# A chunked delta-rule recurrence: turning the inverse's T on VectorE in 32 by 32 blocks, and both directions' products in turn

## The chip, the cores and the metric

The kernel is one program on one core of a Trainium2 chip. The metric is the device time of one execution in microseconds (us). The engines are TensorE (PE; its weight loads are PEld), VectorE (DVE), ScalarE (ACT), GpSimd (POOL) and SyncE (SP), which issues the DMAs here.

## The reference

One layer of a diffusion backbone over 512 latent tokens behind 256 context tokens, in float32: a projection into two token mixers (pooling and a bidirectional RWKV-7 recurrence), a gated merge, and a mixture of experts. Only the recurrence matters here. For each of 16 heads of 64 channels and for both directions it is, token by token:

```python
def step(s, inp):
    r_t, w_t, k_t, v_t, kk_t, b_t = inp
    sa = jnp.einsum('bhvk,bhk->bhv', s, -kk_t)
    s = s * w_t[:, :, None, :] + sa[..., None] * b_t[:, :, None, :] + v_t[..., None] * k_t[:, :, None, :]
    return s, jnp.einsum('bhvk,bhk->bhv', s, r_t)
```

It runs over the context from a zero state and from there over the latent tokens; the second direction runs in reverse.

## The kernel before

The recurrence is worked in chunks of 64 tokens: four of context (0 to 3) and eight latent ones (4 to 11), each with both directions d = 0 and 1. Inside a chunk the steps become matrix products, with the inverse of a 64 by 64 unit triangular matrix per head, T. T begins as the identity with the first off-diagonals (unit T1) and is built up in five levels b = 2, 4, 8, 16, 32: G is a product of the chunk's rows Z with T, X is a product of G with T turned, and a masked copy puts the part of X that belongs to the level into T.

The work of each chunk is a list of units (`recurrence_units`), each with a PSUM bank pair in rotation: unit n takes slot n % 4 and may begin when the reader of unit n - 4 is done (`begin`, `wait_read`). The units are Z (rows of the next chunk, four parts), BKt and Vt (operands turned by a product with the identity), G2 to G32, Tr1 to Tr16 (T turned by TensorE), X2 to X32, and, for the chunk before, P (products with the state), XTr (turned), U (the solved values), Y (output) and S (state update). TensorE goes through them in the written order; chunk i's inverse is interleaved with chunk i - 1's P to S and chunk i + 1's Z. ScalarE and VectorE each read their units in the order of the same list (`by_act`, `by_dve`), and each engine's semaphore (`pe_s`, `act_s`, `dve_s`) counts them.

ScalarE copies Z, Vt (two copies of 64 partitions per direction), BKt, P, XTr, U, every G and every Tr from PSUM to SBUF. VectorE makes T1 (`dve.transpose` of Z in 32 by 32 blocks and a masked copy), the masked copies of X2 to X16 into T, the turned T for the last level (Tf) with X32's masked copy, half of each U, Y's addition and the state update S (an addition and a product with `decay_end`). GpSimd fills T with the identity, clears UV and multiplies Z by its masks once ScalarE has copied it. SyncE loads the rows of the next chunks.

Matrices of 64 by 64 use a quarter of TensorE's array: its row half is given by the operands' partitions, its column half by the output's. `OWN` is the pair of halves of partitions. In G and X the four combinations of row and column half follow one another within one direction, and the row half also picks the PSUM bank of the pair.

## Time and profile before

| what | value |
|---|---|
| median of 3 runs | 1524.66 us (1523.47 to 1525.41) |
| the profiled execution's own time | 1523.53 us |
| its span | 1521.0 us |
| PE busy | 1328.0 us, 87% of the span, 16500 instructions |
| DVE busy | 620.2 us, 41% |
| ACT busy | 578.9 us, 38% |
| POOL busy | 235.3 us, 15% |

The span is the time from the first to the last instruction on the core; the execution's own time holds what lies around it. In the timeline of an engine each row is a run of like instructions: its start, its length from the first start to the last end, the line of the kernel, the operation with output and inputs, the number of instructions, and in brackets how long the engine had stood idle and what ended that. A TensorE matmul of 32-bit data appears as two records, so 32 instructions of G count as x64; the turns with the identity appear once. A row in which the next begins before the first has ended is no error: instructions are pipelined, and start to start is the pace.

### The profile page before, as it was taken

The page shows a single profiled execution, that of the slowest core. Times are in us where ns is not written, and L with a number is a line of the kernel's source. Part 1 is how long each engine was busy: PE and PEld are TensorE (multiplying, and loading weights), DVE is VectorE, ACT ScalarE, POOL GpSimd, SP SyncE. Part 2 cuts the span into 40 slices and gives each one's busy share as a digit, 9 for nine tenths or more (in the row PEclk, how much of TensorE's full clock was granted, in tenths as well). Part 3 has the DMA queues.
Part 4 walks back from the last instruction along what each step waited for, and adds up shares of the span by engine and source line. Part 5 has one row for each costly group of instructions (what it writes and reads, how often), then busy time and mean ns, then how long its engine had stood idle before and what let it go on. Part 6 is the DMA issues. An engine that isn't in the chain of part 4 may idle for free. (4 is left out here: it accounts for less than half of the span.)

```text
span 1521.0 us, 37771 instructions
## 1 busy us (share of the span) xinstructions
PE 1328.0 (87%) x16500; PEld 797.3 (52%) x16500; DVE 620.2 (41%) x974; ACT 578.9 (38%) x964; POOL 235.3 (15%) x191
## 2 busy tenths in 40 slices
PE   5889999999999999999998788999999468788780
PEld 3445555554888888888887233444445323222220
DVE  1247777674555445454444451523321510000014
ACT  4235445542665656556654530000003223322233
POOL 0011111220322333333330000000000011100002
PEclk9999999999999999999999899999999679989895
DMA  9204565645222222112200529453454659999984
GB/s 379 90 1 139 159 174 177 185 123 177 106 86 73 100 67 84 67 71 83 80 29 23 229 99 387 161 202 112 152 219 186 275 214 422 426 424 425 426 341 186
DMA packets 104697, 279.87 MB, mean 184 GB/s; under 512 B 20691, under 2 KB 69971, under 8 KB 90595
## 3 DMA queue, kind: packets, MB, share of 16 engines
q1 hardware_dynamic: 98596, 248.24, 44.0%
q0 software_dynamic: 5952, 29.36, 4.9%
q8 instruction: 127, 2.08, 0.5%
q14 instruction: 22, 0.18, 0.0%
HBM read 232.48 MB, written 53.49 MB: 188 GB/s over the span
## 5 line engine op out<-in xcount | busy, mean ns | idle before, releaser
L391 PE MATMUL pr_ps<-hT,pr_w 128*128 128x512 f32 x384 | 172.2, 602 | 4.0 <-DVEq L99 4.0
L972 DVE COPY_PREDICATED rc_T<-masks_sb,rc_ps 128x512 f32<-128x512 uint32 x96 | 65.2, 728 | 151.2 <-PE rc_ps L761 151.1
L391 PEld LDWEIGHTS pr_ps<-hT,pr_w 128*128 128x128 f32 x384 | 72.1, 191 | 94.9 <-issue 90.1
L1250 PE MATMUL mg_ps<-hT,mg_w 128*128 128x512 f32 x256 | 112.9, 600 | 2.7 <-PEq L1029 2.7
L1737 DVE TENSOR_TENSOR mg_w<-mg_w,ex_pgu 128x256 f32<-128x256 f32 x16 | 6.7, 421 | 194.5 <-ACT mg_w L1731 194.5
L1250 PEld LDWEIGHTS mg_ps<-hT,mg_w 128*128 128x128 f32 x256 | 49.1, 192 | 65.4 <-issue 65.4
L1269 ACT ACTIVATE mg_sig<-mg_ps 128x512 f32<-128x512 f32 x16 | 9.6, 597 | 188.1 <-PE mg_ps L1250 188.1
L761 PE MATMUL rc_ps<-rc_T,rc_Z 64*64 64x64 f32 x3840 | 73.4, 221 | 6.6 <-issue 5.3
L912 ACT ACTIVATE rc_G<-rc_ps 128x512 f32<-128x512 f32 x120 | 66.1, 599 | 23.5 <-PE rc_ps L761 23.0
L501 POOL TENSOR_TENSOR pr_kd<-pr_rate,pool_space 128x768 f32<-128x768 f32 x16 | 29.0, 1814 | 280.9 <-DVE pr_kraw L543 280.9
L734 PE MATMUL rc_ps<-masks_sb,rc_T 128*128 128x128 f32 x480 | 67.6, 281 | 4.8 <-DVE rc_Tf L970 4.8
L936 POOL TENSOR_TENSOR rc_Z<-rc_Z,masks_sb 64x512 f32<-64x512 f32 x48 | 64.9, 1352 | 42.5 <-ACT rc_Z L894 39.7
L761 PEld LDWEIGHTS rc_ps<-rc_T,rc_Z 64*64 64x64 f32 x3840 | 64.4, 135 | 12.7 <-issue 7.9
L894 ACT ACTIVATE rc_Z<-rc_ps 128x1024 f32<-128x1024 f32 (+1 forms) x48 | 41.5, 881 | 74.5 <-PE rc_ps L727 74.5
L914 ACT ACTIVATE rc_Tt<-rc_ps 128x512 f32<-128x512 f32 x120 | 66.8, 609 | 5.3 <-PE rc_ps L734 5.2
L1731 ACT ACTIVATE mg_w<-ex_pgu 128x256 f32<-128x256 f32 x16 | 6.1, 384 | 158.6 <-PE ex_pgu L1869 158.6
L1359 PE MATMUL po_ps<-pl_w_box,merged 128*128 128x512 f32 x128 | 59.5, 621 | 2.8 <-PEq L1205 2.8
L761 PE MATMUL rc_ps<-rc_G,rc_Tt 64*64 64x64 f32 x3072 | 57.4, 221 | 4.0 <-issue 2.3
L1727 ACT ACTIVATE hT<-ex_px,f_cols 128x128 f32<-128x128 f32 x128 | 46.5, 469 | 34.2 <-PE ex_px L1717 34.2
L1250 PE MATMUL mg_ps<-rwkv_y,mg_w 128*128 128x512 f32 x128 | 58.0, 607 | 0.0
L399 PE MATMUL pr_ps<-hT,pr_w 128*128 128x256 f32 x256 | 57.9, 379 | 0.0
L734 PEld LDWEIGHTS rc_ps<-masks_sb,rc_T 128*128 128x128 f32 x480 | 51.2, 141 | 11.0 <-DVE rc_Tf L970 6.4
(358 smaller groups left out, 2596.7 us busy)
## 6 DMA issues: line engine op xcount, KB each, us to landing
bonus_sb<-in_ada_w SPq DMA_DIRECT2D x16, 1024.0 KB, 7.0
mg_w<-in_w_merge SPq DMA_DIRECT2D x8, 1792.0 KB, 7.5
pr_w<-in_w_prep SPq DMA_DIRECT2D x8, 1664.0 KB, 9.8
kr_chunks<-pr_KR SPq DMA_DIRECT2D x16, 768.0 KB, 4.2
bk_chunks<-pr_BK SPq DMA_DIRECT2D x16, 768.0 KB, 6.5
rc_BK<-bk_chunks SPq DMA_DIRECT2D x24, 512.0 KB, 4.2
rc_KR<-kr_chunks SPq DMA_DIRECT2D x24, 512.0 KB, 4.2
rwkv_y<-in_w_experts SPq DMA_DIRECT2D x5, 2048.0 KB, 17.8
```

The source lines that it names most:

```text
L391: last = pe.matmul(lat_bank[:, :], wv[:, j * KT + kt, :], hT[:, kt, lat], start=(kt == 0), stop=(kt == KT - 1))
L399: last = pe.matmul(ctx_bank[:, 0:CTX], wv[:, j * KT + kt, :], hT[:, kt, 0:CTX], start=(kt == 0), stop=(kt == KT - 1))
L734: last = pe.transpose(out[:, q // Q, q % Q * P:q % Q * P + P], src(q), g["ident"])
L761: last = pe.matmul(out[to, k, q * C:q * C + C], lhs(at, q, s, b), rhs(at, q, s, b), start=True, stop=True)
L894: act.activation(Z[u][:, d // 2, :, at:at + Q, 0:w], src.rearrange("p b (j n) -> p b j n", n=P)[:, :, :, 0:w], ACT.Copy).then_inc(act_s, 1)
L912: act.activation(G[:, d, :, :, :], src[:, :, 0:Q * C].rearrange("p s (q t) -> p s q t", q=Q), ACT.Copy).then_inc(act_s, 1)
L914: act.activation(Tt[:, d, :, :, :], turned, ACT.Copy).then_inc(act_s, 1)
L936: pool.tensor_tensor(first, first, both[OWN[side], 0:C].unsqueeze(1).unsqueeze(1).to_broadcast([HD, 2, Q, C]), ALU.mult)
L972: dve.copy_predicated(T[u][:, d, :, :, :].rearrange("p q b t -> p b q t"), level(int(s[1:]), d), by_side).then_inc(dve_s, 1)
L1250: last = pe.matmul(ps[u][j][:, :], w[:, u, w0 + k, :], rhs, start=(k == 0), stop=(k == n - 1))
L1359: last = pe.matmul(ps[t % 2][:, half(h)], merged[:, k, t * P:t * P + P], w[:, k, half(h)], start=(k == 0), stop=(k == KT - 1))
L1727: last = act.activation(xT[:, v, k, :], p_x[:, k, :], ACT.Identity, scale=fcols[:, 0, k:k + 1], bias=fcols[:, 1, k:k + 1])
```

## The change

T is no longer turned by TensorE. After every level VectorE turns it in 32 by 32 blocks (units Tt2 to Tt32), directly behind the masked copy. For direction 0 that is one instruction; for direction 1 it is two, each of 64 partitions, that write the other half of the partitions. The ten Tr units of a chunk and their ScalarE copies are gone, as are Tf and its two turns; X32 is masked straight into the turned T (Tt). Because the two directions' operands or outputs now lie in opposite halves, the products G, X2 to X16 and U go through both directions in turn, and each waits for the second direction's inputs. A direction's outputs of both row halves now share a PSUM bank. X32 is still done direction by direction. The Vt units move from behind G2 to behind U, and U's second half is copied by ScalarE rather than VectorE.

```diff
-        out += front("G2") + front("Tr1") + front("Vt") + back("P")[0:1] + front("X2") + back("P")[1:2]
-        out += front("G4") + front("Tr2") + back("XTr") + front("X4") + back("U")
-        out += front("G8") + front("Tr4") + back("Y") + front("X8") + back("S") + rows_of(0, 1)
-        out += front("G16") + front("Tr8") + rows_of(2) + front("X16") + rows_of(3)
-        out += front("G32") + front("Tr16") + ahead("BKt") + front("X32")
+        out += front("G2") + back("P")[0:1] + front("X2") + back("P")[1:2]
+        out += front("G4") + back("XTr") + front("X4") + back("U") + front("Vt")
+        out += front("G8") + back("Y") + front("X8") + back("S") + rows_of(0, 1)
+        out += front("G16") + rows_of(2) + front("X16") + rows_of(3)
+        out += front("G32") + ahead("BKt") + front("X32")
...
-        if s in ("Z", "Vt", "BKt", "XTr", "U") or s[0] == "G" or s[0:2] == "Tr":
+        if s in ("Z", "Vt", "BKt", "XTr", "U") or s[0] == "G":
...
-        if s == "X32":
-            by_dve += [("turned", i, d)]
-        if s in ("U", "Y", "S") or (s[0] == "X" and s != "XTr"):
+        if s in ("Y", "S") or (s[0] == "X" and s != "XTr"):
             by_dve += [(s, i, d)]
         if s == "Z" and d % 2 == 1:
-            by_dve += [("T1", i, d // 2)]
+            by_dve += [("T1", i, d // 2), ("Tt2", i, d // 2)]
+        if s in ("X2", "X4", "X8", "X16") and d == 1:
+            by_dve += [(f"Tt{2 * int(s[1:])}", i, 0), (f"Tt{2 * int(s[1:])}", i, 1)]
...
-        T, Tf, X = two("T", [Q, 2, C]), sb("Tf", [Q, 2, C]), sb("X", [Q, 2, C])
+        T, Tt, X = two("T", [Q, 2, C]), two("Tt", [Q, 2, C]), sb("X", [Q, 2, C])
         G = sb("G", [2, Q, C])
-        Tt, XT = (sb(nm, [Q, 2, C]) for nm in ("Tt", "XT"))
+        XT = sb("XT", [Q, 2, C])
+        turned_half = lambda d, s: OWN[s if d == 0 else 1 - s]
...
-                def inverse_product(b, i, d):
+                def inverse_product(b, i):
                     u = i % 2
-                    pe.wait_ge(dve_s, dve_at[("T1" if b == 2 else f"X{b // 2}", i, d)])
-                    across(f"G{b}", i, d, lambda at, q, s, h: Z[u][at, d, h, pair_of(q, s), 0:C], lambda at, q, s, h: T[u][at, d, q, h, :], True)
-                def turn_inverse(b, i, d):
-                    turn(f"Tr{b // 2}", i, d, lambda q: T[i % 2][:, d, q, :, :].rearrange("p b t -> p (b t)"))
-                def inverse_update(b, i, d):
-                    pe.wait_ge(act_s, act_at[(f"Tr{b // 2}", i, d)])
-                    of_tt = lambda at, q, s, h: Tt[at, d, q, s, :]
-                    of_g = lambda at, q, s, h: G[at, d, s, q, :]
-                    if b < 32:
-                        across(f"X{b}", i, d, of_tt, of_g, False)
...
+                    pe.wait_ge(dve_s, dve_at[("T1" if b == 2 else f"X{b // 2}", i, 1)])
+                    out = [begin(f"G{b}", i, d) for d in range(2)]
+                    for q in range(Q):
+                        for h in range(2):
+                            for s in range(2):
+                                first, last = (pe.matmul(out[d][turned_half(d, s), h, q * C:q * C + C], Z[u][OWN[s], d, h, pair_of(q, s), 0:C],
+                                                         T[u][OWN[s], d, q, h, :], start=True, stop=True) for d in range(2))
+                    first.then_inc(pe_s, 1)
+                    last.then_inc(pe_s, 1)
+                def inverse_update(b, i):
+                    u = i % 2
+                    pe.wait_ge(act_s, act_at[(f"G{b}", i, 1)])
+                    pe.wait_ge(dve_s, dve_at[(f"Tt{b}", i, 1)])
+                    out = [begin(f"X{b}", i, d) for d in range(2)]
+                    for q in range(Q):
+                        for h in range(2):
+                            for s in range(2):
+                                at = lambda d: turned_half(d, s)
+                                first, last = (pe.matmul(out[d][OWN[s], h, q * C:q * C + C], Tt[u][at(d), d, q, h, :], G[at(d), d, h, q, :],
+                                                         start=True, stop=True) for d in range(2))
+                    first.then_inc(pe_s, 1)
+                    last.then_inc(pe_s, 1)
+                def last_update(i):
+                    u = i % 2
+                    pe.wait_ge(act_s, act_at[("G32", i, 1)])
+                    pe.wait_ge(dve_s, dve_at[("Tt32", i, 1)])
+                    for d in range(2):
+                        out = begin("X32", i, d)
+                        for q in range(Q):
+                            for h in range(2):
+                                for half in OWN:
+                                    last = pe.matmul(out[half, h, q * C:q * C + C], G[half, d, h, q, :], Tt[u][half, d, q, h, :], start=True, stop=True)
+                        last.then_inc(pe_s, 1)
...
-                def solved(k, d):
-                    pe.wait_ge(act_s, act_at[("XTr", k, d)])
-                    pe.wait_ge(dve_s, dve_at[("X32", k, d)])
-                    out = begin("U", k, d)
+                def solved(k):
+                    pe.wait_ge(act_s, act_at[("XTr", k, 1)])
+                    pe.wait_ge(dve_s, dve_at[("X32", k, 1)])
+                    out = [begin("U", k, d) for d in range(2)]
                     for q in range(Q):
                         for h in range(2):
                             for s in range(2):
-                                last = pe.matmul(out[OWN[s], 0, (2 * q + h) * C:(2 * q + h) * C + C], Tf[OWN[s], d, q, h, :], X[OWN[s], d, q, h, :], start=True, stop=True)
+                                at = lambda d: turned_half(d, s)
+                                first, last = (pe.matmul(out[d][OWN[s], 0, (2 * q + h) * C:(2 * q + h) * C + C], Tt[k % 2][at(d), d, q, h, :],
+                                                         X[at(d), d, q, h, :], start=True, stop=True) for d in range(2))
+                    first.then_inc(pe_s, 1)
                     last.then_inc(pe_s, 1)
...
-                    pe.wait_ge(dve_s, dve_at[("U", k, d)])
...
+                        if front:
+                            inverse_product(b, i)
                         for d in range(2):
-                            if front:
-                                inverse_product(b, i, d)
-                        for d in range(2):
-                            if front:
-                                turn_inverse(b, i, d)
-                        for d in range(2):
-                            if b == 2 and front:
-                                turn_v(i, d)
-                            elif b == 4 and back:
+                            if b == 4 and back:
...
@@ -863,14 +883,18 @@
                             state(k, 0)
                         if b == 16 and ahead:
                             rows_of(n, 2)
-                        for d in range(2):
-                            if front:
-                                inverse_update(b, i, d)
+                        if front:
+                            if b < 32:
+                                inverse_update(b, i)
+                            else:
+                                last_update(i)
                         if b == 2 and back:
                             state(k, 1)
+                        if b == 4 and back:
+                            solved(k)
                         for d in range(2):
-                            if b == 4 and back:
-                                solved(k, d)
+                            if b == 4 and front:
+                                turn_v(i, d)
                             elif b == 8 and back and k < CHUNKS - 1:
                                 state_update(k, d)
...
-                        act.activation(UV[u][0:HD, d, 1::2, :, :], turned[0:HD], ACT.Copy).then_inc(act_s, 1)
+                        act.activation(UV[u][0:HD, d, 1::2, :, :], turned[0:HD], ACT.Copy)
+                        act.activation(UV[u][HD:P, d, 0::2, :, :], turned[HD:P], ACT.Copy).then_inc(act_s, 1)
...
-                    elif s[0:2] == "Tr":
-                        act.activation(Tt[:, d, :, :, :], turned, ACT.Copy).then_inc(act_s, 1)
...
                     if i >= 2:
-                        pool.wait_ge(pe_s, pe_at[("Tr16", i - 2, 1)])
-                        pool.wait_ge(dve_s, dve_at[("turned", i - 2, 1)])
+                        pool.wait_ge(pe_s, pe_at[("G32", i - 2, 1)])
+                        pool.wait_ge(dve_s, dve_at[("Tt32", i - 2, 1)])
...
-                    elif s == "turned":
+                    elif s[0:2] == "Tt":
+                        if s == "Tt2" and i >= 2:
+                            dve.wait_ge(pe_s, pe_at[("U", i - 2, 1)])
                         dve.drain()
-                        dve.transpose(Tf[:, d, :, :, :].rearrange("p q b t -> p (q b t)"), T[u][:, d, :, :, :].rearrange("p q b t -> p (q b t)")).then_inc(dve_s, 1)
+                        for half, to in ((slice(0, P), slice(0, P)),) if d == 0 else zip(OWN, OWN[::-1]):
+                            last = dve.transpose(Tt[u][to, d, :, :, :].rearrange("p q b t -> p (q b t)"), T[u][half, d, :, :, :].rearrange("p q b t -> p (q b t)"))
+                        last.then_inc(dve_s, 1)
                     elif s == "X32":
-                        dve.drain()
-                        dve.copy_predicated(Tf[:, d, :, :, :].rearrange("p q b t -> p b q t"), level("32t", d), by_side).then_inc(dve_s, 1)
+                        dve.copy_predicated(Tt[u][:, d, :, :, :].rearrange("p q b t -> p b q t"), level("32t", d), by_side).then_inc(dve_s, 1)
...
-                    elif s == "U":
-                        turned = src[:, 0, :].rearrange("p (q b t) -> p q b t", q=Q, b=2)
-                        dve.tensor_copy(UV[u][HD:P, d, 0::2, :, :], turned[HD:P]).then_inc(dve_s, 1)
```

On VectorE, in a context chunk (a latent one has Y's two additions ahead of these), from the masked copies of X8 to the state updates; before the change:

```order
L972 COPY_PREDICATED rc_T<-masks_sb,rc_ps 128x2x4x64 x2
L983 TENSOR_TENSOR rc_S<-rc_S,rc_ps 128x512
L985 TENSOR_TENSOR rc_S<-rc_S,decay_end 128x512
L983 TENSOR_TENSOR rc_S<-rc_S,rc_ps 128x512
L985 TENSOR_TENSOR rc_S<-rc_S,decay_end 128x512
```

and after it, where L1000 is the masked copies of X8, L995 the turns of T for the next level, L1008 and L1010 the state update:

```order
L1000 COPY_PREDICATED rc_T<-masks_sb,rc_ps 128x2x4x64 x2
L995 STREAM_TRANSPOSE rc_Tt<-rc_T 128x512
L995 STREAM_TRANSPOSE rc_Tt<-rc_T 64x512 x2
L1008 TENSOR_TENSOR rc_S<-rc_S,rc_ps 128x512
L1010 TENSOR_TENSOR rc_S<-rc_S,decay_end 128x512
L1008 TENSOR_TENSOR rc_S<-rc_S,rc_ps 128x512
L1010 TENSOR_TENSOR rc_S<-rc_S,decay_end 128x512
```

The state updates now stand behind three turns of T.

Right behind these come T1 of the next chunk's direction 0, X16, T1 of direction 1 and X32; before the change:

```order
L961 STREAM_TRANSPOSE rc_XT<-rc_Z 64x512 x2
L964 COPY_PREDICATED rc_T<-masks_sb,rc_XT 128x2x4x64
L972 COPY_PREDICATED rc_T<-masks_sb,rc_ps 128x2x4x64 x2
L961 STREAM_TRANSPOSE rc_XT<-rc_Z 64x512 x2
L964 COPY_PREDICATED rc_T<-masks_sb,rc_XT 128x2x4x64
L967 STREAM_TRANSPOSE rc_Tf<-rc_T 128x512
L970 COPY_PREDICATED rc_Tf<-masks_sb,rc_ps 128x2x4x64
L967 STREAM_TRANSPOSE rc_Tf<-rc_T 128x512
L970 COPY_PREDICATED rc_Tf<-masks_sb,rc_ps 128x2x4x64
```

and after it, where L986 and L989 are T1, L995 the turns, L1000 and L998 the masked copies of X16 and X32:

```order
L986 STREAM_TRANSPOSE rc_XT<-rc_Z 64x512 x2
L989 COPY_PREDICATED rc_T<-masks_sb,rc_XT 128x2x4x64
L995 STREAM_TRANSPOSE rc_Tt<-rc_T 128x512
L1000 COPY_PREDICATED rc_T<-masks_sb,rc_ps 128x2x4x64 x2
L995 STREAM_TRANSPOSE rc_Tt<-rc_T 128x512
L995 STREAM_TRANSPOSE rc_Tt<-rc_T 64x512 x2
L986 STREAM_TRANSPOSE rc_XT<-rc_Z 64x512 x2
L989 COPY_PREDICATED rc_T<-masks_sb,rc_XT 128x2x4x64
L995 STREAM_TRANSPOSE rc_Tt<-rc_T 64x512 x2
L998 COPY_PREDICATED rc_Tt<-masks_sb,rc_ps 128x2x4x64 x2
```

X16's copies stand behind one turn more and X32's behind three more and two less, all in one queue.

On ScalarE, from the copies of G4 to those of G8; before the change:

```order
L912 ACTIVATE rc_G<-rc_ps 128x512 x2
L914 ACTIVATE rc_Tt<-rc_ps 128x512 x2
L908 ACTIVATE rc_X<-rc_ps 128x512 x2
L910 ACTIVATE rc_UV<-rc_ps 64x4x128 x2
L912 ACTIVATE rc_G<-rc_ps 128x512 x2
```

and after it, where L939 is G, L934 XTr, L936 and L937 the two halves of U, L920 and L921 those of Vt:

```order
L939 ACTIVATE rc_G<-rc_ps 128x512 x2
L934 ACTIVATE rc_X<-rc_ps 128x512 x2
L936 ACTIVATE rc_UV<-rc_ps 64x4x128
L937 ACTIVATE rc_UV<-rc_ps 64x4x128
L936 ACTIVATE rc_UV<-rc_ps 64x4x128
L937 ACTIVATE rc_UV<-rc_ps 64x4x128
L920 ACTIVATE rc_UV<-rc_ps 64x4x128
L921 ACTIVATE rc_UV<-rc_ps 64x4x128
L920 ACTIVATE rc_UV<-rc_ps 64x4x128
L921 ACTIVATE rc_UV<-rc_ps 64x4x128
L939 ACTIVATE rc_G<-rc_ps 128x512 x2
```

G8's copies now stand behind eight copies of 64 partitions.

## Rows read from the trace of the kernel before

**Rows 1.** The windows: busy us of each engine, granted clock, DMA share, GB/s.

```profile
389.00:832.80 443.80, 416.56 (x12754) 381.77 (x12752) 217.80 (x295) 260.97 (x443) 132.62 (x93) 1.00 0.20 71
614.30:633.70 19.40, 17.61 (x581) 16.18 (x572) 14.72 (x20) 11.46 (x17) 12.51 (x8) 1.00 0.16 57
902.00:908.00 6.00, 4.38 (x7) 2.00 (x8) 1.22 (x2) 1.28 (x1) 2.23 (x4) 0.74 0.60 196
```

**Rows 2.** TensorE's timeline where the state products of direction 0 (and one of direction 1) begin.

```profile
418.31 1.15 PE L746 MATMUL rc_ps<-rc_KR,rc_S 64*64 64x64 f32 x32
...
421.45 1.12 PE L746 MATMUL rc_ps<-rc_KR,rc_S 64*64 64x64 f32 x32
...
557.95 1.96 PE L746 MATMUL rc_ps<-rc_KR,rc_S 64*64 64x128 f32 x32
...
788.55 1.96 PE L746 MATMUL rc_ps<-rc_KR,rc_S 64*64 64x128 f32 x32
...
819.11 1.96 PE L746 MATMUL rc_ps<-rc_KR,rc_S 64*64 64x128 f32 x32
```

**Rows 3.** TensorE's timeline: S, G16 and Tr8, Z, P of direction 1, U.

```profile
617.35 1.85 PE L822 MATMUL rc_ps<-rc_UV,rc_BKt 128*64 128x64 f32 x55 [1.20 <-issue]
...
621.11 1.16 PE L761 MATMUL rc_ps<-rc_T,rc_Z 64*64 64x64 f32 x64
622.21 1.09 PE L734 MATMUL rc_ps<-masks_sb,rc_T 128*128 128x128 f32 x8
623.23 1.16 PE L727 MATMUL rc_ps<-rc_KR,rc_BK 64*128 64x128 f32 x16
...
822.90 1.96 PE L746 MATMUL rc_ps<-rc_KR,rc_S 64*64 64x128 f32 x32
...
828.43 2.08 PE L805 MATMUL rc_ps<-rc_X,rc_Tf 64*64 64x64 f32 x64 [0.32 <-ACT rc_X L908]
```

**Rows 4.** VectorE's timeline from X8's copies to the first turn into Tf.

```profile
615.57 1.33 DVE L972 COPY_PREDICATED rc_T<-masks_sb,rc_ps 128x512 f32<-128x512 uint32 x2
618.30 0.69 DVE L983 TENSOR_TENSOR rc_S<-rc_S,rc_ps 128x512 f32<-128x512 f32 x1 [1.40 <-PE rc_ps L822]
...
620.43 0.69 DVE L985 TENSOR_TENSOR rc_S<-rc_S,decay_end 128x512 f32<-128x512 f32 x1
622.31 1.43 DVE L961 STREAM_TRANSPOSE rc_XT<-rc_Z 64x512 f32<-64x512 f32 x2 [1.18 <-PE rc_ps L761]
623.81 1.77 DVE L964 COPY_PREDICATED rc_T<-masks_sb,rc_XT 128x512 f32<-128x512 uint32 x1
...
629.18 0.77 DVE L964 COPY_PREDICATED rc_T<-masks_sb,rc_XT 128x512 f32<-128x512 uint32 x1
630.04 0.71 DVE L967 STREAM_TRANSPOSE rc_Tf<-rc_T 128x512 f32<-128x512 f32 x1
```

**Rows 5.** ScalarE's timeline: G4, two of Vt's copies, the first of U's in the last chunk.

```profile
605.20 1.09 ACT L912 ACTIVATE rc_G<-rc_ps 128x512 f32<-128x512 f32 x2
...
635.43 0.59 ACT L897 ACTIVATE rc_UV<-rc_ps 64x512 f32<-64x512 f32 x1
636.05 0.59 ACT L896 ACTIVATE rc_UV<-rc_ps 64x512 f32<-64x512 f32 x1
...
829.63 0.59 ACT L910 ACTIVATE rc_UV<-rc_ps 64x512 f32<-64x512 f32 x1 [0.76 <-PE rc_ps L805]
```

**Rows 6.** GpSimd's timeline: the masking products of direction 0.

```profile
622.36 2.60 POOL L936 TENSOR_TENSOR rc_Z<-rc_Z,masks_sb 64x512 f32<-64x512 f32 x2 [1.16 <-ACT rc_Z L894]
625.10 2.68 POOL L940 TENSOR_TENSOR rc_Z<-rc_Z,masks_sb 128x1024 f32<-128x1024 f32 x1
```

**Rows 7.** TensorE's timeline: BKt at the first chunk, and two stops.

```profile
385.62 3.67 PE L734 MATMUL rc_ps<-masks_sb,rc_BK 128*128 128x128 f32 x16
...
466.29 1.03 PE L761 MATMUL rc_ps<-rc_T,rc_Z 64*64 64x64 f32 x53 [1.39 <-issue]
...
903.62 15.67 PE L1250 MATMUL mg_ps<-hT,mg_w 128*128 128x512 f32 x32 [2.71 <-PEq L1029]
```

15 lines of the change are left out of this document (6 added, 9 removed).

## The prediction

> **What bounds the kernel now.** I read the windows first, then TensorE's timeline, then the other engines' timelines in one chunk. Between 389.0 and 832.8 us the recurrence runs alone, and TensorE is busy 416.56 of 443.80 us at a granted clock of 1.00, VectorE 217.80, ScalarE 260.97 [rows 1]. So TensorE's queue sets the time there. The starts of the state products P give the pace [rows 2]: 557.95 and 788.55 are the first and last of seven such starts, so six stretches with latent chunks take 230.60 / 6 = 38.4 us each; the four before them take (557.95 - 418.31) / 4 = 34.9; the last stretch between two P takes 819.11 - 788.55 = 30.6. That TensorE is the bound says what removed TensorE work could be worth at most. But VectorE is not evenly idle: from the X8 copies to the X32 copies (614.3 to 633.7) it is busy 14.72 of 19.40 us [rows 1]. There its queue follows TensorE closely, and there the change puts most of its new work.
>
> **What is removed.** The Tr units: 8 transposes for both directions, from 622.21 to 623.23, so 1.02 us, five times a chunk: 5.1 us of TensorE [rows 3]. A product with four 64 by 64 tiles in turn (both directions) takes 622.21 - 621.11 = 1.10 us; the diagonal one, U, takes about 1.96 (its 64 records from 828.43 need 2.08 with the end of the last) [rows 3]. U now gets four tiles, and X32 becomes diagonal: -0.9 and +0.9, nothing. So 5.1 us a chunk, 61 us over twelve, if nothing waits. ScalarE loses ten copies of Tr and VectorE loses the two Tf turns and two U copies.
>
> **What is added to VectorE.** Per level 0.71 us for direction 0 (the existing turn of 128x512, [rows 4]) and two turns of 64 partitions for direction 1, 1.43 us as the two at 622.31, with a drain before each of about 0.08 (623.81 less the end of 622.31's, 623.74) [rows 4]. That is 2.3 us a level, 11.5 a chunk, against 1.4 and 1.4 removed.
>
> **The chain after the change.** I follow one latent chunk from the start of P of direction 0 to the next, in two halves. A hand-over from the last issue of a product to its reader is about 0.25 us: U of direction 0 is issued in half of 1.96 from 828.43, and ScalarE starts at 829.63 [rows 3, 5].
>
> First half, TensorE and ScalarE. P takes 822.90 - 819.11 = 3.79 us per direction [rows 2, 3]. P, X2, P put G4 at 8.7. X4 now waits for both G4 copies, two in 1.09 us [rows 5]: 8.7 + 1.1 + 0.25 + 1.09 = 11.1 (the XTr turns of 1.0 lie inside). X4 and U: 13.3. Then ScalarE has U's four copies of 64 partitions and behind them Vt's four, which moved here. The old Vt copies start 0.61 apart (635.43, 636.05) [rows 5], so eight take 4.9: 18.5. G8's two copies come behind them: 19.6. X8 and its hand-over end at 20.9. TensorE's own work between U and X8 (Vt, G8, Y, about 3.2) is hidden under this, with some 3 us of stall: G8 cannot begin before U's bank is read, Y not before Vt's, X8 not before ScalarE has done all of them. In the old order X8 was issued 3.5 us after U.
>
> Second half, VectorE, one queue in order: two X8 copies 1.33, turns for level 16 2.3, two S updates 2.82 (618.30 to 620.43 plus 0.69), T1 of direction 0 1.43 + 0.08 + 0.77, its turn 0.79, two X16 copies 1.33, turns for level 32 2.3, T1 of direction 1 2.28, its two turns 1.51, X32's first copy 0.73: 17.7 us [rows 4]. The next P takes the bank of X32 direction 0, so it starts behind that copy. X16's copies wait some 0.7 more for TensorE and ScalarE, since G16 takes S's banks and so begins behind the S updates: 1.1 + 0.25 + 1.09 + 1.1 + 0.25 = 3.8 against 3.1 of VectorE's own. That makes 18.4.
>
> The period is 20.9 + 18.4 = 39.3 us, where 38.4 stands now. The removed 5.1 is more than eaten by 5.4 us of turns in the second half (2.3 + 0.8 + 2.3) that sit one behind another with S, T1 and the copies, by Tt2 of direction 1 (1.5), and by the ScalarE queue after U.
>
> **Two costs of unknown size.** The port: T1's masked copy reads two operands from SBUF. It took 1.77 us at 623.81, started in GpSimd's second masking product of 622.36 and ended 0.6 after that had ended; at 629.18, between two of GpSimd's instructions, it took 0.77, while the turn at 630.04 took 0.71 under a running one [rows 4, 6]. So the turns don't suffer and the masked copies do. After the change T1 comes later than GpSimd's start, and its copy falls about where GpSimd's next instruction of 2.68 us starts (2.74 after its first, [rows 6]). Nothing if VectorE is just ahead, up to 2.8 us a chunk if just behind. Because the last S update with decay_end reads SBUF twice too and meets the first masking product, I take behind: 2.0 us in latent chunks and 1.5 in context chunks, which have only the 1.3 us pieces. This is what the Trainium skill says in SBUF — State Buffer, "SBUF: two separate sides": a VectorE instruction with two SBUF inputs and a reading GpSimd instruction lock each other out for a whole instruction; the trace agrees (1.77 against 0.77).
> The pauses: TensorE stops now and then inside a product with nothing to wait for, 1.20 us before 617.35 and 1.39 before 466.29 [rows 3, 7]. They cost their full length in a saturated queue, about 1 us a chunk, and are already in the 38.4. In the new chain half of TensorE's time is off the path: 0.5 us a chunk, bounds 0 and 1.5.
>
> **The sum.** Latent: 39.3 + 2.0 + 0.5 = 41.8, that is +3.4, six times: +20.4. Context: P of 64 columns takes 421.45 - 418.31 less X2's 1.0, so 2.15 in place of 3.79, twice: 39.3 - 3.3 = 36.0, + 1.5 + 0.5 = 38.0 against 34.9: +3.1, four times: +12.4. Last stretch: no T1 and no Z, but five levels now bare; 20.9, then 12.4 (X8 copies 1.4, G16 and its copies to X16 2.5, S on VectorE to 6.5, X16 copies to 7.9, G32 to X32 2.5, X32 1.96), with 0.5 of pause 33.8: +3.2. Start and tail, where both directions now end together and a bare level takes about 5.2 (1.1 + 0.25 + 1.09 + 1.1 + 0.25 + 1.33 and three hand-backs) : about +2. Together +38. The profiled execution took 1523.53 us around its span of 1521.0, 1.1 under the median of 1524.66; so 1561.5 for it and 1563 for the median. Nothing outside the recurrence changes.
>
> **Rivals.**
> The turns are hidden: VectorE is busy only 217.80 of 443.80 us [rows 1]. If they fell into its pauses the removed 5.1 us would show, 12 x 5.1 = 61: 1464. It decides on whether the second half is shorter than TensorE's work beside it (S 1.9, Z 4.0, G16, X16, G32 3.3, BKt 1.9, X32 and G2 3.0: 14.1). It is 17.7, so the new 5.4 would have to be 1.5 instead; against it. Chance 0.07, and 0.04 for a draw.
> The clock: TensorE now stands still for about 3 us before G16 in each chunk. After a stop of 2.71 us before 903.62 the granted clock was 0.74 in 902 to 908, so partly at 1.2 in place of 2.4 GHz; after one of 1.39 us before 466.29 it was not (the recurrence stands at 1.00) [rows 1, 7]. At the low level BKt took 3.67 us for 16 (385.62), against about 1.9 [rows 7]. Products of 1.1 us would cost 0.9 more, two of them on the path: 1.8 x 11 = 20, so 1583. Chance 0.18.
> The banks: in the new G and X products the two halves of rows write one PSUM bank at once, in different partitions, where before each half had its bank. If that took away the fourfold overlap, each of nine products would take U's 1.96: 9 x 0.9 x 12 = 97, part of it hidden: about 1650. The Trainium skill speaks for it: TensorEngine Tiling (Array Packing), "Gotcha 1: PSUM Pressure", says that different row tiles cannot access the same bank at the same time. Against it: U did write from both row halves into one bank, and issued one record in 0.031 us, as the S product with only column tiles (55 in 1.85) [rows 3]; no penalty shows. Chance 0.04.
>
> **How the numbers follow.** The forecast as told has 0.62: its own range is 1538 (no port, no pauses: 0.9 x 6 + 1.1 x 4 + 2.7 + 2) to 1583 (port 2.8 and pauses 1.5 throughout). The remaining 0.05 is a slower case that I don't see. The range to 1592 takes in about half of the clock rival, and the low end is 1536, leaving out the faster, equal and bank cases. Faster by over 0.2% (about what a measurement here can tell from no change) 0.07, within 0.2% 0.04, slower 0.89.
>
> **What the profile after would show.** Right: VectorE's rows from the X8 copies to the X32 copies back to back, about 18 to 21 us; TensorE stopped 2 to 3.5 us before G16, released by rc_S; a stop before G8 and X8 released by rc_UV and rc_G; periods between P starts of about 42 and 38; T1's masked copy at 1.8 us or more. Wrong: periods under 38, or idle time of VectorE in that stretch; clock under 1.00 in the recurrence would speak for the second rival; product rows of 1.9 us for the third. What I would have got wrong then is most likely how long ScalarE's eight copies hold X8, or a port wait that falls out of step and vanishes.

## The result, and the profile after

The changed kernel takes 1599.34 us (median of 4, 1595.24 to 1605.70) against 1524.07 for the kernel before beside it: ratio 1.0501, 95% interval 1.0462 to 1.0541. That is 75 us slower; the forecast was 39 slower (1563, range 1536 to 1592). Sign and main mechanism were right, the size was half of what came. The profiled execution has a span of 1598.4 us. The page's first lines, then the windows of the recurrence and of 12 us in one latent chunk (columns as in [rows 1]):

```profile
span 1598.4 us, 36803 instructions
PE 1316.4 (82%) x16020; PEld 784.1 (49%) x16020; DVE 719.1 (45%) x1106; ACT 534.6 (33%) x868; POOL 233.4 (15%) x191
```

```profile
388.40:906.60 518.20, 405.56 (x12272) 369.64 (x12272) 315.37 (x424) 216.40 (x347) 129.66 (x93) 0.90 0.17 60
741.00:753.00 12.00, 8.52 (x206) 8.12 (x209) 6.61 (x10) 1.94 (x2) 2.31 (x3) 0.72 0.18 65
```

The recurrence takes 518.2 us where it took 443.8 [rows 1]; TensorE is busy 11 us less in it, VectorE 98 more, and the granted clock is 0.90 where it was 1.00. Six latent stretches take 45.3 us each (forecast 41.8), four context stretches 41.3 (38.0), the last 37.1 (33.8). Their starts in TensorE's timeline, answering [rows 2]:

```profile
417.33 1.15 PE L749 MATMUL rc_ps<-rc_KR,rc_S 64*64 64x64 f32 x32 [0.84 <-DVE rc_Tt L998]
...
721.01 1.96 PE L749 MATMUL rc_ps<-rc_KR,rc_S 64*64 64x128 f32 x32 [1.20 <-DVE rc_Tt L998]
...
766.26 1.96 PE L749 MATMUL rc_ps<-rc_KR,rc_S 64*64 64x128 f32 x32 [1.21 <-DVE rc_Tt L998]
```

The chunk from 721.01 takes 45.25 us. Its first half on TensorE, from G8 to G16 (to be held against [rows 3]):

```profile
736.77 1.16 PE L774 MATMUL rc_ps<-rc_T,rc_Z 64*64 64x64 f32 x64 [1.40 <-ACT rc_UV L937]
738.01 0.69 PE L763 MATMUL rc_ps<-rc_Z,rc_UV 64*64 64x64 f32 x32
739.24 0.69 PE L763 MATMUL rc_ps<-rc_Z,rc_UV 64*64 64x64 f32 x32 [0.54 <-ACT rc_UV L921]
740.35 0.46 PE L789 MATMUL rc_ps<-rc_G,rc_Tt 64*64 64x64 f32 x15 [0.41 <-ACT rc_G L939]
743.80 1.64 PE L789 MATMUL rc_ps<-rc_G,rc_Tt 64*64 64x64 f32 x49 [3.00 <-issue]
745.38 3.68 PE L848 MATMUL rc_ps<-rc_UV,rc_BKt 128*64 128x64 f32 x64
748.99 2.42 PE L730 MATMUL rc_ps<-rc_KR,rc_BK 64*128 64x128 f32 x32
752.08 1.16 PE L774 MATMUL rc_ps<-rc_T,rc_Z 64*64 64x64 f32 x64 [0.68 <-DVE rc_S L1010]
```

X8 begins 740.35 - 721.01 = 19.3 us after P; forecast 19.6. The stops before G8, Y and X8 are the ones named, released by ScalarE's UV and G copies. Two things were not in the sum. TensorE stands still for 3.00 us inside X8 with nothing to wait for, and the S product behind it takes 3.68 us, where the first 55 of its 64 records took 1.85 before [rows 3]: the clock is at its lower level (0.72 granted on average from 741 to 753). The second half on VectorE, answering [rows 4]:

```profile
745.41 1.35 DVE L1000 COPY_PREDICATED rc_T<-masks_sb,rc_ps 128x512 f32<-128x512 uint32 x2 [4.74 <-PE rc_ps L789]
746.86 2.23 DVE L995 STREAM_TRANSPOSE rc_Tt<-rc_T 128x512 f32<-128x512 f32 x3
749.12 0.69 DVE L1008 TENSOR_TENSOR rc_S<-rc_S,rc_ps 128x512 f32<-128x512 f32 x1
...
752.53 1.42 DVE L986 STREAM_TRANSPOSE rc_XT<-rc_Z 64x512 f32<-64x512 f32 x2 [0.59 <-ACT rc_Z L918]
754.03 1.75 DVE L989 COPY_PREDICATED rc_T<-masks_sb,rc_XT 128x512 f32<-128x512 uint32 x1
755.87 0.71 DVE L995 STREAM_TRANSPOSE rc_Tt<-rc_T 128x512 f32<-128x512 f32 x1
756.51 1.32 DVE L1000 COPY_PREDICATED rc_T<-masks_sb,rc_ps 128x512 f32<-128x512 uint32 x2
757.92 2.23 DVE L995 STREAM_TRANSPOSE rc_Tt<-rc_T 128x512 f32<-128x512 f32 x3
760.18 1.43 DVE L986 STREAM_TRANSPOSE rc_XT<-rc_Z 64x512 f32<-64x512 f32 x2
761.68 2.15 DVE L989 COPY_PREDICATED rc_T<-masks_sb,rc_XT 128x512 f32<-128x512 uint32 x1
763.93 1.43 DVE L995 STREAM_TRANSPOSE rc_Tt<-rc_T 64x512 f32<-64x512 f32 x2
765.38 1.33 DVE L998 COPY_PREDICATED rc_Tt<-masks_sb,rc_ps 128x512 f32<-128x512 uint32 x2
```

This is the closed queue of the forecast: from the X8 copies (24.4 us after P, forecast 20.9) to the next P 20.85 us, with 0.6 idle. T1's masked copies take 1.75 and 2.15 us against the 0.77 of an undisturbed one [rows 4], 2.4 too much together (forecast 2.0). So this chunk is 20.9 + 3.5 + 20.85: the excess is the stop of 3.0 and half a us of slow X8. Over the six latent stretches it is much the same. Split at the start of X8's first copy, the six take 23.9 us before it (forecast 20.9) and 21.4 after it (forecast 18.4 + 2.0, and 0.5 of pauses somewhere): of the 3.5 us that each is over the forecast, 3.0 lie in the first half, which holds 2.5 us of stops without a releaser.

### The profile page after: what moved, and what is told of

Its sections match the earlier page's. It is cut to its first block and busy times, and to the rows that moved or that the text cites. A ratio compares the mean times of both kernels' runs of the same rounds, so it can differ in the third digit from the quotient of the medians.

```text
span 1598.4 us, 36803 instructions
## 1 busy us (share of the span) xinstructions
PE 1316.4 (82%) x16020; PEld 784.1 (49%) x16020; DVE 719.1 (45%) x1106; ACT 534.6 (33%) x868; POOL 233.4 (15%) x191
## 5 line engine op out<-in xcount | busy, mean ns | idle before, releaser
L995 DVE STREAM_TRANSPOSE rc_Tt<-rc_T 128x512 f32<-128x512 f32 (+1 forms) x180 | 127.4, 708 | 12.4 <-issue 0.4
L1000 DVE COPY_PREDICATED rc_T<-masks_sb,rc_ps 128x512 f32<-128x512 uint32 x96 | 64.3, 723 | 132.4 <-PE rc_ps L789 132.4
L939 ACT ACTIVATE rc_G<-rc_ps 128x512 f32<-128x512 f32 x120 | 65.1, 595 | 78.4 <-PE rc_ps L774 77.9
L789 PE MATMUL rc_ps<-rc_G,rc_Tt 64*64 64x64 f32 x3072 | 65.5, 237 | 28.8 <-ACT rc_G L939 16.5
L918 ACT ACTIVATE rc_Z<-rc_ps 128x1024 f32<-128x1024 f32 (+1 forms) x48 | 41.5, 881 | 113.0 <-PE rc_ps L730 112.9
L789 PEld LDWEIGHTS rc_ps<-rc_G,rc_Tt 64*64 64x64 f32 x3072 | 57.7, 148 | 37.3 <-ACT rc_G L939 22.7
L961 POOL TENSOR_TENSOR rc_Z<-rc_Z,masks_sb 64x512 f32<-64x512 f32 x48 | 61.7, 1285 | 55.1 <-ACT rc_Z L918 52.8
L730 PE MATMUL rc_ps<-rc_KR,rc_BK 64*128 64x128 f32 (+1 forms) x768 | 59.6, 308 | 1.5 <-DMA rc_KR<-kr_chunks 1.5
```

What stands on the lines that cost most here:

```text
L730: last = pe.matmul(out[:, b, j * P:j * P + w], BK[at, d, p, :, :].rearrange("p j t -> p (j t)"), KR[u][at, d, p, :, :].rearrange("p j t -> ...
L789: first, last = (pe.matmul(out[d][OWN[s], h, q * C:q * C + C], Tt[u][at(d), d, q, h, :], G[at(d), d, h, q, :], start=True, stop=True) for ...
L939: act.activation(G[:, d, :, :, :], src[:, :, 0:Q * C].rearrange("p s (q t) -> p s q t", q=Q), ACT.Copy).then_inc(act_s, 1)
L961: pool.tensor_tensor(first, first, both[OWN[side], 0:C].unsqueeze(1).unsqueeze(1).to_broadcast([HD, 2, Q, C]), ALU.mult)
L995: last = dve.transpose(Tt[u][to, d, :, :, :].rearrange("p q b t -> p (q b t)"), T[u][half, d, :, :, :].rearrange("p q b t -> p (q b t)"))
L1000: dve.copy_predicated(T[u][:, d, :, :, :].rearrange("p q b t -> p b q t"), level(int(s[1:]), d), by_side).then_inc(dve_s, 1)
```

## The experiments

All times are medians in us; the ratio is to the kernel before, run beside each. That one's own median was between 1524.1 and 1528.0, so the gain of one variant over another comes out some us larger by the ratios than by the medians. Recurrence, its TensorE stops without a releaser ("pauses", 0.3 us or more) and its time at the lower clock are from one profiled execution.

```
kernel          time   ratio (95% interval)      recurrence  pauses  low clock
before         1524.1  1                             443        17       0
after          1599.3  1.0501 (1.0462 to 1.0541)     518        22      99
vt_back        1585.5  1.0405 (1.0382 to 1.0428)     505        21     106
vt_u_back      1587.3  1.0426 (1.0395 to 1.0457)     501        22      75
turns_late     1592.7  1.0476 (1.0425 to 1.0527)     507        25      75
fill           1603.5  1.0518 (1.0477 to 1.0559)     518        31      58
tt2_out        1584.5  1.0361 (1.0324 to 1.0398)     505        25     116
kr_first       1597.8  1.0467 (1.0429 to 1.0504)     515        13     113
after_tiny     1587.3  1.0386 (1.0353 to 1.0419)     508         9      89
before_tiny    1520.4  0.9946 (0.9931 to 0.9960)     439        12       0
combo          1574.8  1.0313 (1.0279 to 1.0346)     494        24      99
fill512        1610.9  1.0538 (1.0504 to 1.0572)     529        28      68
tiny_fill      1583.3  1.0369 (1.0342 to 1.0395)     503        17       7
half_masks     1589.2  1.0427 (1.0389 to 1.0464)     504        24      96
before_joined  1552.7  1.0167 (1.0142 to 1.0193)     474        18       0
hybrid         1566.1  1.0241 (1.0215 to 1.0267)     488        43      48
hybrid_kr      1533.1  1.0039 (1.0024 to 1.0054)     452        27       7
```

### Parts of the change taken back

**vt_back** puts Vt behind G2 again.

```diff
-        out += front("G4") + back("XTr") + front("X4") + back("U") + front("Vt")
+        out += front("G2") + front("Vt") + back("P")[0:1] + front("X2") + back("P")[1:2]
+        out += front("G4") + back("XTr") + front("X4") + back("U")
```

> The changed kernel with Vt back behind G2. Chain theory: ScalarE's queue between U and X8 loses four of its eight copies of 64 partitions (4 x 0.61 = 2.4 us a chunk), and the first half of the chain gets that much shorter: 11 x 2.4 = 27 us, so about 1572 where the changed kernel has 1599. Clock theory (the 36 us by which the result lies above the chain's 1563 come from TensorE at half clock behind its stops): the stops before G8 and X8 shrink as well, the granted clock rises from the 0.90 of the recurrence, and the gain is larger than the queue's, 35 to 55 us. Rival, the turns on VectorE alone are the bound: no gain, under 8 us.

13 us came back by the medians (15 by the ratios), half of the 27 expected. X8 moves from 19.3 to about 18 us behind P, but Vt (1.9 us) now stands between X32's copies and P: VectorE's second half plus that is 22 to 24 us instead of 20.5 to 21. What leaves the ScalarE queue in one half comes back on TensorE in the other.

**vt_u_back** also gives U's second half back to VectorE.

```diff
+        if s in ("U", "Y", "S") or (s[0] == "X" and s != "XTr"):
-                        act.activation(UV[u][HD:P, d, 0::2, :, :], turned[HD:P], ACT.Copy).then_inc(act_s, 1)
+                        dve.tensor_copy(UV[u][HD:P, d, 0::2, :, :], turned[HD:P]).then_inc(dve_s, 1)
```

> The same, and the second half of each U copied by VectorE again. Chain theory: two more copies of 0.61 leave ScalarE's queue behind U (1.2 us a chunk) and two of 0.69 join VectorE's queue where it is otherwise idle, behind X4's turns: another 11 x 1.2 = 13 us, so about 1559. Clock theory: the stop before G8 is then gone and the clock stays up in that stretch, so 20 us or more. Rival: VectorE is the bound and gets longer, 0 to 15 us slower than vt_back.

No difference to vt_back, where another 13 us were expected.

**turns_late** issues VectorE's turns for level 16 behind the S updates, and direction 0's for level 2 behind X16's copies.

> The changed kernel with only VectorE's order changed: the turns for level 16 stand behind the state updates instead of ahead of them, and the level 2 turn of direction 0 behind X16's copies. Chain theory: G16 no longer waits for 2.3 us of turns, and X16's copies not for 0.8: 3.1 us a chunk, 11 x 3.1 = 34 us, so about 1565, with the stop before G16 down from 2.7 us to under 1. Clock theory: the stop before G16 goes, but the ones before G8 and X8 remain and take the clock down as before; 34 us or a little more. Rival, ScalarE's queue after U is the whole cost: under 8 us.

7 us by the medians where 34 were expected; the intervals overlap. The second half of a latent stretch went from 21.4 to 20.7 us, not down by 3.1: in a queue that is nearly full from X8's copies to X32's, exchanging members gains little. **tt2_out** takes members out of that stretch:

```diff
-            by_dve += [("T1", i, d // 2), ("Tt2", i, d // 2)]
+            by_dve += [("T1", i, d // 2)]
+        if s == "X32" and d == 1 and i + 1 < CHUNKS:
+            by_dve += [("Tt2", i + 1, 0), ("Tt2", i + 1, 1)]
```

> In the changed kernel the turns for level 2 of the next chunk (0.77 + 1.75 us) stand on VectorE behind the last copies of level 32 instead of ahead of the second direction's T1, so they are beside the first product of the next chunk and P. If VectorE's nearly closed queue from X8's copies to X32's is what sets the second half, 2.3 us a chunk come off: 12 x 2.3 = 27, time 1572 (1565 to 1580). Against it: the first update of level 2 now waits for these turns (X32's copies, then 2.5 us, while G2 and its copies take 3.5): no price. Rival (the period is set by the ScalarE and TensorE chain, VectorE's queue has slack): 1595 to 1602.

15 us by the medians (21 by the ratios), where 27 were expected: the latent stretches fall from 45.3 to 43.3, their second half from 21.4 to 19.9 (2.3 were expected off), and the time at the lower clock rises by 17 us. **combo** is vt_u_back and tt2_out together.

> The changed kernel with two edits together that each gained alone: Vt behind G2 again with U's second half copied by VectorE (1587), and the turns for level 2 behind X32's copies (1584.5). One shortens the first half of a chunk, the other VectorE's queue in the second half, so the gains should add: 1599 - 12 - 15 = 1572 (1566 to 1578). Rival (both gains were clock spells and not chain): no sum, 1582 to 1590.

The two gains add as expected (12 + 15, measured 25, all by the medians). This is the quickest form of the whole change, and still 3.1% slower than the kernel before.

**before_joined** is one part of the change alone: in the kernel before, G and X of levels 2 to 16 and U go through both directions in turn; the turns stay on TensorE.

```diff
+                def joined(stage, i, lhs, rhs, there):
+                    out = [begin(stage, i, d) for d in range(2)]
+                    for q in range(Q):
+                        for s in range(2):
+                            for b in range(2):
+                                last = []
+                                for d in range(2):
+                                    s_, b_ = s ^ d, b ^ d
...
-                    pe.wait_ge(dve_s, dve_at[("T1" if b == 2 else f"X{b // 2}", i, d)])
+                    pe.wait_ge(dve_s, dve_at[("T1" if b == 2 else f"X{b // 2}", i, 1)])
```

> The kernel before with one part of the change alone: both directions' products of a level are issued in turn, 2 to 16 and U's (direction 1 in the opposite halves), and so start when the later direction's operand is there and end together. All turns stay on TensorE. Theory: TensorE has the turns and other work between product and update, so most copies stay hidden; the first direction's result comes 1.1 us later at 10 places of a chunk, of which some lie on the chain: 0 to 2 us a chunk, time 1525 to 1550, likeliest 1535. Rival (products in turn use two halves of the array at once and are quicker than one after the other): rows below 1.16 us and a time below 1522.

25 us slower, just past the slow end of what was expected (1525 to 1550, likeliest 1535). That is a third of the whole loss, without a single turn on VectorE and at a full clock; whether this part costs the same inside the changed kernel was not tested. Products are no quicker for going in turn (1.16 us as before), and every level now waits for the later direction. Three of its TensorE rows, X4, G32 and the next chunk's G2, each with such a wait:

```profile
623.36 1.16 PE L773 MATMUL rc_ps<-rc_G,rc_Tt 64*64 64x64 f32 x64 [0.35 <-ACT rc_Tt L933]
...
643.40 1.33 PE L773 MATMUL rc_ps<-rc_T,rc_Z 64*64 64x64 f32 x64 [0.41 <-DVE rc_T L991]
...
648.80 1.16 PE L773 MATMUL rc_ps<-rc_T,rc_Z 64*64 64x64 f32 x64 [0.21 <-ACT rc_BKt L918]
```

**half_masks** prices the port: GpSimd's second masking product is left out (its part of the computation too).

> The changed kernel without GpSimd's second mask product of each direction (the 128x1024 one over the output part of Z; that part of the computation is left out), to price what GpSimd's passes cost VectorE: T1's masked copies take 1.77 and 2.2 to 2.7 us beside GpSimd here and 0.77 alone. Port theory: the second half of a latent chunk, VectorE's closed queue, falls by 0.5 to 1.5 us, 7 chunks, time 1599 to 1588 to 1596, with T1's copies at 0.8 to 1.6. Rival (no share of it lies on the chain): 1597 to 1601.

The direction 1 copy of T1 now meets no GpSimd work and takes 0.75 us; direction 0's, still beside the first product, takes 1.75 as before:

```profile
702.32 1.75 DVE L985 COPY_PREDICATED rc_T<-masks_sb,rc_XT 128x512 f32<-128x512 uint32 x1
...
709.95 0.75 DVE L985 COPY_PREDICATED rc_T<-masks_sb,rc_XT 128x512 f32<-128x512 uint32 x1
```

```profile
700.87 2.60 POOL L961 TENSOR_TENSOR rc_Z<-rc_Z,masks_sb 64x512 f32<-64x512 f32 x2 [1.17 <-ACT rc_Z L918]
705.88 2.60 POOL L961 TENSOR_TENSOR rc_Z<-rc_Z,masks_sb 64x512 f32<-64x512 f32 x2 [2.41 <-ACT rc_Z L918]
```

The time fell by 10 us by the medians, as the port theory had it, though the two intervals just touch; 1.4 us in each of eight chunks would be 11. The second half shows it more clearly: in five of the six latent stretches it takes 19.3 to 19.9 us, where the changed kernel had 20.5 to 21.2 (the sixth, 24.3, has 3.5 us of pauses and 10 us at the lower clock in it). So direction 1's masked copy is on the path; direction 0's was not tested.

### Pauses and clock

**fill** computes Vt, Y and two of the Z parts twice, to keep TensorE busy.

> The changed kernel with more TensorE work and nothing taken away: Vt, Y and the second Z part of each direction are computed twice (the second pass writes the same values again), some 5 us a chunk, put where TensorE stood still: before G8, before X8, before G16 and before G32. Chain theory without a clock term: the time does not fall; 0 to 20 us slower, as far as the repeats are longer than the stops. Clock theory: the granted clock in the recurrence goes to 0.97 or more and the time falls by 10 to 30 us although more is computed.

It gained nothing, and fits neither theory: the lower clock fell from 99 to 58 us, yet the time did not fall. The added instructions brought more pauses (31 us, up to 4.9 each), and part of the added work lay on the path.

**after_tiny** and **before_tiny** cut the later chunks' row loads to 16 elements a partition.

```diff
+                        n = 16 if i >= (1 if dst is BK else 2) else KT * 2 * C
-                        sp.dma_start(dst[:, d, :, :, :].rearrange("p i b t -> p (i b t)"),
+                        sp.dma_start(dst[:, d, :, :, :].rearrange("p i b t -> p (i b t)")[:, 0:n],
```

> The changed kernel, but the row loads of the later chunks (BK, KR, V) fetch 16 elements of each partition instead of 512 or 256, so the later chunks compute with left-over rows (that part of the computation is left out); every instruction, wait and semaphore stays. Theory A (the pauses of TensorE's own queue, 22 us over the recurrence with the longest of 3.0 us, come where the row loads and the y store fill the DMA engines just when the next 16 KB of TensorE's instructions should come): the pauses fall to below 5 us, the half-clock spells that follow them become fewer, time 1599 to about 1560 to 1575. Theory B (pauses are the rate of TensorE's own instructions, whatever else the DMA engines carry): pauses stay at 15 to 25 us, time 1590 to 1600. Theory C (the half clock comes from the waits for VectorE alone): pauses fall, the clock of the recurrence stays at 0.90, time about 1580.

> The same cut of the later chunks' row loads in the kernel before (the same part of the computation is left out). Theory A: its pauses, 16.6 us with none above 1.4, fall to below 5 us; the time falls by 8 to 15 us from 1525, so that the gap between the two kernels without row loads is that of the chain alone, 45 to 60 us. Theory B: nothing changes, 1523 to 1526. If this kernel gains as much as the changed one, the pauses are no part of the loss of 75 us.

The pauses fell from 22 to 9 us (theory A said below 5), the longest from 3.0 to 1.6. So the row loads lengthen them. But the time fell by 12 (18 by the ratios), not by 24 or more: the lower clock stayed (89 us, granted clock 0.91), as theory C said, though theory C had 1580. The kernel before gained 8, so of the 75 us the loads explain some 4 to 9. Where the 3.00 us stop stands, SyncE had issued V and KR in one go and y's store 3 us later, because KR's load had to queue behind the wait for Vt (SyncE's timeline):

```profile
735.41 0.80 SPq L676 DMA_DIRECT2D rc_V<-v_chunks  x2
736.26 0.90 SPq L671 DMA_DIRECT2D rc_KR<-kr_chunks  x2
739.48 0.33 SPq L681 DMA_DIRECT2D y_chunks<-rc_yc  x1
```

Before, the KR load went out at 604.22 of a chunk begun at 595.53, and y's store 11 us later. The DMA view of 735 to 745 has the DMA engines 57% busy with rows, and in it two packets of a queue of kind "instruction":

```profile
q1 hardware_dynamic: 720, 1.84, 57.1%
q8 instruction: 2, 0.03, 1.3%
```

The packets' own times say more. TensorE stopped from 740.80 to 743.80; one 16 KB packet of that queue moved from 741.34 to 742.30, and TensorE went on 1.5 us later. All 23 pauses of the kernel before and all 14 of the changed one end in this way, 1.1 to 1.6 us behind the landing of such a packet, though the packets come only every 4 to 5 us. In the kernel before, every one of these packets had set out before TensorE stopped. In the changed kernel the three longest stops (2.5, 2.7 and 3.0 us) are those whose packet set out only after TensorE had stopped.

**kr_first** issues KR's load ahead of the wait for Vt.

```diff
-                        sp.wait_ge(pe_s, pe_at[("Vt", i - 1, 1)])
-                        load_v(i)
                     if i >= 2 and i < CHUNKS:
                         sp.wait_ge(pe_s, pe_at[("P", i - 2, 1)])
                         load_pairs(KR[i % 2], g["kr_dram"], i, kr_loaded[i % 2])
+                    if i < CHUNKS:
+                        sp.wait_ge(pe_s, pe_at[("Vt", i - 1, 1)])
+                        load_v(i)
```

> In the changed kernel SyncE issues the KR load (512 KB a direction) as soon as P of the chunk before has read it, ahead of the wait for Vt and the V load, instead of behind them; nothing else moves. Theory A (row loads and the y store that start together starve TensorE of its next instructions): the longest pauses (3.0 us inside X8) go, pauses 22 to 12 to 16 us, some half-clock spells with them, time 1599 to 1575 to 1588. Theory B (where the loads stand does not matter): 1595 to 1602. Cost of the move itself: SyncE and the DMA queues only, none on the chain.

Pauses fell to 13 us as theory A said, and the time stayed where theory B had it (the intervals overlap). It does hold the cleanest latent chunk of the design, with no lower clock and one pause of 0.28 us; its S product takes 2.09 us, not 3.68:

```profile
672.34 1.96 PE L750 MATMUL rc_ps<-rc_KR,rc_S 64*64 64x128 f32 x32 [1.21 <-DVE rc_Tt L999]
...
692.18 1.16 PE L790 MATMUL rc_ps<-rc_G,rc_Tt 64*64 64x64 f32 x64 [0.41 <-ACT rc_G L940]
694.58 2.09 PE L849 MATMUL rc_ps<-rc_UV,rc_BKt 128*64 128x64 f32 x64 [1.24 <-DVE rc_T L1001]
...
700.03 1.16 PE L775 MATMUL rc_ps<-rc_T,rc_Z 64*64 64x64 f32 x64 [1.38 <-DVE rc_S L1011]
...
713.87 0.33 PE L750 MATMUL rc_ps<-rc_KR,rc_S 64*64 64x128 f32 x2 [1.21 <-DVE rc_Tt L999]
```

The stretch behind it, also without a pause and with 3.4 us at the lower clock, takes 43.1 us. Its first half is 0.3 us shorter, but VectorE's second half, back to back, is 1.9 longer, 1.2 of it in T1's two copies, the first of which begins 0.13 behind the start of a GpSimd product of 2.35 us:

```profile
743.00 2.82 DVE L990 COPY_PREDICATED rc_T<-masks_sb,rc_XT 128x512 f32<-128x512 uint32 x1
...
751.84 2.67 DVE L990 COPY_PREDICATED rc_T<-masks_sb,rc_XT 128x512 f32<-128x512 uint32 x1
```

So where T1 falls beside GpSimd's products decides how long it waits. In after_tiny and kr_first the two copies together take 5.5 us in seven of the twelve latent stretches, against 3.9 in the changed kernel, and the second half is then 22.3 to 22.6 us long. That takes back part of what fewer pauses give.

The clean chunk takes 713.87 - 672.34 = 41.5 us, against the forecast's 41.8, of which 0.5 was for pauses. Over the 18 latent stretches of after, after_tiny and kr_first a least-squares fit gives 41.7 (+- 0.3) + 0.37 (+- 0.03) x time at the lower clock + 0.35 (+- 0.08) x pauses, with 0.5 us left over. The 0.35 nets the pauses against the port, since stretches with a pause in the first half mostly have the shorter T1 copies. Fitted to the first half alone, up to X8's first copy, the same stretches give 21.1 + 0.26 (+- 0.04) x lower clock + 0.76 (+- 0.09) x pauses. The fits are correlations, and nothing was varied alone in them: of the 43.1 us stretch above, the first one would put 1.3 us on the lower clock where the rows show the port.

**fill512** adds products of 128x512 in TensorE's waits, into unread parts of PSUM.

```diff
+                    if b in (8, 16):
+                        filler({8: "U", 16: "S"}[b], i - 1, {8: 2, 16: 3}[b])
+                    elif b in (2, 32):
+                        begin(f"G{b}", i, 0)
+                        filler(f"G{b}", i, {2: 2, 32: 1}[b])
```

> The changed kernel with filler products for TensorE in its waits: 8 products of 128x128 by 128x512 of constants a chunk, about 0.5 us each, before G2 (2), G8 (2), G16 (3) and G32 (1), into parts of PSUM that nobody reads; few instructions, so few more to fetch, and no wait changes. Clock theory (a chunk costs 41.7 us + 0.37 of its time at half clock + 0.35 of its pauses, by a fit over the latent chunks of three variants; TensorE's idle time brings the half clock): time at half clock in the recurrence falls from 99 us to below 40, time 1599 to 1575 to 1585. Rival (the half clock does not hang on these waits; the filler only delays): low clock stays at 80 to 115 us, time 1600 to 1612.

Neither theory as stated. A filler took 0.94 us, twice the expected length, so G16 came up to 1 us later; the lower clock fell only to 68 us. In the latent stretches its spells began during, or within 1.3 us of, stops of 1.2 to 4.0 us in Y or X8. Whether the clock costs anything by itself was left open; **tiny_fill** has both edits:

> The changed kernel with both edits: the later chunks' row loads cut to 16 elements a partition (their part of the computation is left out) and 8 filler products of 128x512 a chunk in TensorE's waits. Theory (pauses and waits together bring the half clock, and it costs 0.37 of its length): half clock in the recurrence from 89 us (loads cut alone) and 68 us (filler alone) to below 25 us, pauses below 10; latent chunks of 42 to 43 us, that is the chain plus up to 1 us of filler that delays G16; time 1570 to 1582. Rival (the half clock comes whatever fills the waits): 60 us or more at half clock, time 1588 to 1600.

Its window of the recurrence, then after_tiny's, then fill512's:

```profile
390.90:893.80 502.90, 449.89 (x12451) 364.16 (x12450) 322.38 (x422) 215.25 (x346) 129.49 (x92) 0.99 0.03 8
```

```profile
390.20:898.50 508.30, 400.88 (x12272) 365.74 (x12272) 325.52 (x424) 215.53 (x346) 130.15 (x93) 0.91 0.03 8
```

```profile
390.90:919.50 528.60, 468.65 (x12451) 382.68 (x12450) 318.01 (x422) 215.19 (x346) 127.80 (x92) 0.94 0.18 59
```

The lower clock is gone (7 us, 0.99) only with both, though 17 us of pauses are left, twice what was expected, none over 1.9. The latent stretches take 42.6 us on average, as expected, though each holds 7.5 us more of filler and G16 waits for some of it. So either of the two, the unfilled waits (89 us) or the row loads with their long stops (68 us), is enough for most of the lower clock. For its price the pair fill512 and tiny_fill is the closest test, since they differ only in the row loads: 61 us less at the lower clock and 11 us less of pauses came with 28 us less time. At the fit's 0.37 and 0.35 this would be 27. But 18 us fewer of the pauses fall into first halves; at 0.76 they make 14 of the 28, and about 0.2 of its length is left for the lower clock. The loads alone were worth 8 in the kernel before, which had no lower clock. Against after_tiny the gain is only 4 us and the intervals overlap, since the filler costs something too. The total missed the expected range by 1 us on the slow side: a context stretch takes 41.5 us, 1.1 more than in after_tiny, although at full clock; that the filler lies on the path there is likely, not shown.

### VectorE's turns only where VectorE has room

**hybrid** is the kernel before with VectorE's turns at levels 4 and 8 alone.

```diff
-        out += front("G2") + front("Tr1") + front("Vt") + back("P")[0:1] + front("X2") + back("P")[1:2]
-        out += front("G4") + front("Tr2") + back("XTr") + front("X4") + back("U")
-        out += front("G8") + front("Tr4") + back("Y") + front("X8") + back("S") + rows_of(0, 1)
+        out += front("G2") + front("Tr1") + back("P")[0:1] + front("X2") + back("P")[1:2]
+        out += front("G4") + back("XTr") + ([] if late else front("Vt")) + front("X4") + back("U")
+        out += front("G8") + (front("Vt") if late else []) + back("Y") + front("X8") + back("S") + rows_of(0, 1)
+        if s in ("X2", "X4") and d == 1:
+            by_dve += [(f"Tv{2 * int(s[1:])}", i, 0), (f"Tv{2 * int(s[1:])}", i, 1)]
```

> The kernel before, with VectorE's turns for levels 4 and 8 alone (there both directions' products go in turn as in the change and TensorE's Tr2 and Tr4 with their ScalarE copies are gone); levels 2, 16 and 32 are turned by TensorE as before, and VectorE's copy of U's second half stays. Vt moves into the room of the turns that are gone: ahead of X4 in the latent chunks that have no Y, else as the waits allow. VectorE has gaps in the first half of a chunk in the kernel before, so its 4 turns (2.5 us a level) lie beside G4 and G8 and lengthen nothing; TensorE loses 2 x 2.2 us of turns a chunk and gains waits of 1 to 2 us. Theory (the change is bad only where it loads VectorE's closed queue, from X8's copies on): faster than before by 0.5 to 1%, 1510 to 1518. Rival (TensorE's waits bring pauses and half clock here too, so nothing is won): 1525 to 1545, with low-clock time above 20 us in the recurrence.

39 us slower than before, beyond the theory and beyond the rival's 1545 as well, most of it in the context chunks (43.3 us against 34.9). There KR's load left at 525.75 behind the wait for Vt, and Z's product waited for it (a wait for a DMA that the timeline shows as "issue"):

```profile
523.49 2.21 SPq L678 DMA_DIRECT2D rc_V<-v_chunks  x2
525.75 0.91 SPq L673 DMA_DIRECT2D rc_KR<-kr_chunks  x2
```

```profile
531.66 3.65 PE L732 MATMUL rc_ps<-rc_KR,rc_BK 64*128 64x128 f32 x31 [4.16 <-issue]
```

**hybrid_kr** issues KR's load first, as kr_first does.

> hybrid with one edit: SyncE issues the KR load of the next chunk as soon as P of the chunk before has read it, ahead of the wait for Vt and the V load. Theory (in hybrid's context chunks, 43.3 us against 34.9 before, Z's products wait for a KR load issued 8 us too late): the context chunks fall to 35 to 37 us, 4 x 7 = 28 less, time 1566 to 1538 (1532 to 1545), pauses from 43 us to about 20, no half clock there. It stays slower than before, since its latent chunks take 39.9 us against 38.4. Rival (the gap in the context chunks is the half clock's and the queue's own): 1555 to 1567.

```profile
388.10:840.20 452.10, 402.22 (x12561) 366.42 (x12560) 266.31 (x366) 238.01 (x395) 132.68 (x93) 0.99 0.20 69
```

33 us came back with one load moved, as the theory had it (1533 in a range of 1532 to 1545), and the clock with it. TensorE is busy 14 us less than before and the recurrence still takes 9 us more: the latent stretches 38.8 (38.4 before), the context ones 36.2 (34.9). So even where VectorE has room, removing TensorE work did not pay, in the one arrangement that was tried. No kernel here beat the one before (before_tiny leaves rows out).

## Why the prediction was right and wrong

**What bounds the kernel; removed and added work.** Right. TensorE lost its work and the time rose, since the chain through VectorE's queue took over.

**First half, 19.6 to X8 and 20.9 to its copies.** Right: X8 at 19.3, and its copies at 20.5 to 20.7 where neither pause nor lower clock falls in (chunks of after_tiny and kr_first).

**Second half, 18.4 + port 2.0.** Right for the changed kernel: 20.5 to 21.2 us nearly back to back in five of the six latent chunks (in the sixth, 24.2, S and Z ran at the lower clock), T1's copies 2.4 us too long; half_masks confirms GpSimd's product as the cause of 1.4 of it. That the port's wait depends on where T1 falls was said, and after_tiny and kr_first show it: up to 3.9 us too long there, above the 2.8 that the forecast had as its most.

**The chain's sum, 41.8 latent.** Right for a clean chunk, which should be 41.3 without the pauses: 41.5 measured (one chunk), 41.7 by the fit. For the context chunks the clean value was, by the same kind of fit over 12 stretches, 36.9 +- 0.8 against 38.0 (37.5 without the pauses); all twelve had some time at the lower clock, so this one is extrapolated, and the quickest took 38.4.

**Pauses, 0.5 a chunk, bounds 0 and 1.5.** Too small, and for a wrong reason: half of TensorE's time was taken to be off the path, but in the latent chunks 2.5 of the 2.7 us of pauses fell before X8's copies, where TensorE and ScalarE are the path. At 0.35 they cost 0.9 a chunk, at the first half's 0.76 about 1.9. Over the whole recurrence the first halves hold 19 us of them: 15 us at 0.76, where the sum had 5.5. Single stops of 3.0 us were outside what the recurrence of before shows (1.4 at most). What makes them long fits V, KR and y's store going out close together behind the moved Vt; that follows from the order of SyncE's queue, and I did not follow SyncE past the move.

**The clock: this is the step that failed.** The likeliest case was summed at a full clock, so the clock stood in the sum at nothing, and was a rival at 0.18 and 20 us. Measured are 99 us at the lower level. At 0.37 of their length, the latent chunks' 6.8 us each cost 2.5, the context chunks' 12 about 4 (0.34 by their fit): 6 x 2.5 + 4 x 4 = 31 us of the 36 that were missing. That is an estimate and rather the upper end: at the 0.2 that fill512 against tiny_fill leaves, the 99 us cost 20, and the pauses have some 9 more than the sum gave them. No run changed the clock alone. So the clock has 20 to 31 us of the gap and the pauses most of the rest. Two errors: its chance (the stops before G8 and X8 and those of 2 to 3.5 us before G16 were forecast for every chunk, and a stop of 2.7 us with a lower clock behind it stood in [rows 7]), and its price (two products of 1.1 us were charged; 12 of the 14 spells last 6.8 us or more, and they also cover S, 3.68 for 2.09, and Z, which the second half waits for). tiny_fill shows the chain without it: the same waits filled and the loads gone, clock 0.99, 42.6 us a chunk.

**Rivals.** Turns hidden: refuted, VectorE had 0.6 us of idle time in the second half of the chunk shown. Banks: refuted, G and X take 1.16 us with both row halves in one bank, as before. That is against the rule of the Trainium skill, TensorEngine Tiling (Array Packing), "Gotcha 1: PSUM Pressure", so far as it would cost time here.

**Not in the prediction as a cost of its own:** the products in turn, +25 us when they are the only change (before_joined). It was inside the chain's sum, but I did not see it as a part.

**Open:** what brings the clock down in a given chunk (in the changed kernel the stretch from 766.26 has 5.5 us of pauses and no lower clock, the one from 674.54 no pause and 10 us of it), how the 36 us divide exactly between clock, pauses and port, and whether another order with turns at levels 4 and 8 beats the kernel before.

## What to carry to other kernels

When a change takes an engine from saturated to waiting, sum the chain twice, once at each level of the clock, and weigh the second by how many stops the first one makes. Work taken off the busiest engine was worth nothing here, since it joined a queue that was already nearly closed, and making two independent directions wait for each other had a price even before anything else changed. Follow a moved step through the DMA queue too: a load behind a later wait cost 33 us in hybrid and showed only as "issue".

## What was not expected of the hardware

Row loads lengthen TensorE's stops without a releaser: with them cut, 22 us became 9 and the longest 3.0 became 1.6; in the kernel before 17 became 12. Each of the 37 pauses of the two kernels ends 1.1 to 1.6 us behind the landing of a 16 KB packet of kind "instruction", so what TensorE waits for there is, by all 37, its next instructions. That the row loads are what delays these packets fits the runs with the loads cut; it was not isolated.

No single condition accounts for the lower clock. Unfilled waits with the loads cut gave 89 us of it, filled waits with the loads 68, filled waits with the loads cut 7; and the kernel before with products in turn, some 30 us of waits and 18 us of stops in 474, none of these over 1.7, had none.
